# Prompt masks added on VectorE, in one operation with the queries' factor and the maximum, in a hybrid decoder step on one core

## The reference, cut to what matters

```python
logits = jnp.einsum('qngd,qknd->qngk', qg, ks).astype(jnp.float32) * (HEAD_DIM ** -0.5)
logits = jnp.where(valid[:, None, None, :], logits, -jnp.inf)
p = jax.nn.softmax(logits, axis=-1).astype(vs.dtype)
return jnp.einsum('qngk,qknd->qngd', p, vs).reshape(n_q, H_A * HEAD_DIM)
```

## Time and profile before

| | |
|---|---|
| median of 3 runs | 643.3 us (642.88 to 644.36) |
| profiled execution, own time | 640.95 us |
| its span | 639.3 us |
| granted TensorE clock | 1.00 |
| busy: TensorE, VectorE, ScalarE, GpSimd | 98%, 64%, 47%, 24% of the span |
| attention steps 8 to 23 | 287 to 375 us of the span |

### The profile page before, as it was taken

The page is one execution under the profiler, slowest core; times in us unless marked ns, Lnnn a source line. Parts: engine busy times, 40 slices in busy tenths (PEclk is TensorE's granted clock), DMA queues, the critical chain, the costliest instruction groups (busy, mean ns, idle before and its releaser), DMA issues.

```text
span 639.3 us, 13025 instructions
## 1 busy us (share of the span) xinstructions
PE 628.2 (98%) x4822; PEld 608.6 (95%) x4822; DVE 408.8 (64%) x671; ACT 298.3 (47%) x480; POOL 156.4 (24%) x211
## 2 busy tenths in 40 slices
PE   8999999999999999999999999999999999999998
PEld 6999999999999998888878899999999999999998
DVE  5765656565455568486999738868565656564441
ACT  7644444444334356455545667555444444443330
POOL 1477775000011227367412200260000000000000
PEclk9999999999999999999999999999999999999999
DMA  8777676545544556534232324544545454555530
GB/s 327 259 229 242 198 237 201 188 129 184 179 169 156 171 168 209 183 117 129 67 108 91 103 97 136 187 140 165 164 142 188 138 191 137 182 150 193 177 107 19
DMA packets 34906, 104.79 MB, mean 164 GB/s; under 512 B 6064, under 2 KB 8752, under 8 KB 34864
## 3 DMA queue, kind: packets, MB, share of 16 engines
q1 hardware_dynamic: 30432, 97.98, 46.3%
q0 software_dynamic: 3616, 4.73, 2.4%
q10 hardware_dynamic: 816, 1.51, 0.7%
HBM read 100.21 MB, written 1.70 MB: 159 GB/s over the span
## 4 chain that ended last, share of the span: by engine, by line
PE 86%; DVE 4%; DMA 2%; ACT 2%; SPq 2%; POOL 2%; issue 1%; ACTq 0%; POOLq 0%
PE ps L1190 27%; PE ps L1192 26%; PE ps L1191 26%; DVE wlo L863 1%; SPq L485 1%; DMA x<-in_x 1%; ACT whi L626 1%; PE ps L1322 1%; DVE acc L1034 1%; PE ps L1354 1%; PE ps L1385 1%; PE ps L1395 1%; DMA kv<-kv 1%; PE ps L1306 1%; PE ps L1214 0%
## 5 line engine op out<-in xcount | busy, mean ns | idle before, releaser
L863 DVE TENSOR_TENSOR wlo<-raw,whi 128x1024 fp32r<-128x1024 f32 (+2 forms) x180 | 221.3, 1234 | 125.8 <-ACT whi L626 125.5
L1190 PE MATMUL ps<-nhi,whi 128*128 128x288 f32 (+1 forms) x944 | 283.3, 300 | 1.6 <-DVE kv L1093 0.8
L1191 PE MATMUL ps<-nlo,whi 128*128 128x288 f32 (+1 forms) x944 | 278.5, 295 | 0.0
L1192 PE MATMUL ps<-nhi,wlo 128*128 128x288 f32 (+1 forms) x944 | 277.6, 294 | 0.0
L626 ACT ACTIVATE whi<-raw 128x1024 fp32r<-128x1024 f32 (+2 forms) x180 | 181.2, 1029 | 120.8 <-PE ps L1192 106.7
L1190 PEld LDWEIGHTS ps<-nhi,whi 128*128 128x128 f32 (+1 forms) x944 | 176.5, 187 | 6.7 <-issue 2.6
L1192 PEld LDWEIGHTS ps<-nhi,wlo 128*128 128x128 f32 (+1 forms) x944 | 177.4, 188 | 0.0
L1191 PEld LDWEIGHTS ps<-nlo,whi 128*128 128x128 f32 (+1 forms) x944 | 176.9, 187 | 0.3
L1190 PE MATMUL ps<-hhi,whi 128*128 128x288 f32 x336 | 99.5, 296 | 0.0
L1191 PE MATMUL ps<-hlo,whi 128*128 128x288 f32 x336 | 99.1, 295 | 0.0
L1192 PE MATMUL ps<-hhi,wlo 128*128 128x288 f32 x336 | 98.8, 294 | 0.0
(11 more groups left out here) (185 smaller groups left out, 681.5 us busy)
## 6 DMA issues: line engine op xcount, KB each, us to landing
raw<-in_weights SPq DMA_DIRECT2D x164, 512.0 KB, 3.5
raw<-in_weights SPq DMA_DIRECT2D x16, 384.0 KB, 3.4
raw<-in_weights SPq DMA_DIRECT2D x4, 256.0 KB, 5.4
kt<-in_cache_kidx_a POOLq DMA_DIRECT2D x32, 32.0 KB, 3.0
kt<-in_cache_k_b POOLq DMA_DIRECT2D x16, 64.0 KB, 3.1
kt<-in_cache_k_a POOLq DMA_DIRECT2D x32, 32.0 KB, 3.0
vb_pg<-in_cache_v_b POOLq DMA_DIRECT2D x16, 64.0 KB, 3.3
cst<-in_constants ACTq DMA_DIRECT2D x1, 948.0 KB, 7.9
```

Of the source, the lines that this page charges most:

```text
L863: nc.vector.tensor_tensor(wlo[:, v % NU, 0:nk, 0:w], raw[:, v % NR, 0:nk, 0:w], whi[:, v % NU, 0:nk, 0:w].bitcast(F32), ALU.subtract).then ...
L1190: nc.tensor.matmul(out[0:w, 0:N], h, hi, start=start and i == 0, stop=False)
L1191: nc.tensor.matmul(out[0:w, 0:N], h, lo, start=False, stop=False)
L1192: ins = nc.tensor.matmul(out[0:w, 0:N], l, hi, start=False, stop=stop and done is not False and i == len(ks) - 1)
```

## The change

The mask matmuls of the prompt steps are gone; the heads' matmuls start their banks themselves. VectorE takes each head's logits out of PSUM, adds the mask from SBUF, multiplies by the negated factor (`rq_neg`, made once for each kind at steps 8 and 16) and takes the minimum, all in one operation that writes the result to `probs` and the minimum to `nmax`. There is one such operation per head, two in a step of form 1 and four in form 0, where one reduction and one small product covered all heads of a step. ScalarE makes the exponential in place in `probs`, with scale -1. The searches write their masks in fp32 over `acc1` and `acc0`. The bf16 copies `idb`, `causalb`, `sel1` and `sel0` and their casts are gone. The sample steps (form 2) keep their mask matmuls and the reduction.

The waits follow: VectorE waits for the top-k mask and for the transposes of the step two before (its buffer of `probs`), TensorE waits for VectorE's maxima of the pair before in place of its exponentials; up to step 8 and at step 16 it still waits for the exponentials.

```diff
@@ logits (TensorE)
-                if m:
+                if 0 < m <= 8 or m in (16, 24):
                     pe.wait_ge(soft_done, m)
+                elif m:
+                    pe.wait_ge(max_done, m - 8)
...
-                if kind == DSA and i == 0:
-                    pe.wait_ge(sel_ready, {1: 1, 0: 2, 2: 3}[form])
+                if kind == DSA and form == 2:
+                    pe.wait_ge(sel_ready, 3)
...
-                    if kind != IDX:
-                        mask = ((causalb[:] if kind == MOBA else sel1[:]) if form == 1
-                                else (causalb[:, P:2 * P] if kind == MOBA else sel0[:]))
-                        for bank in banks:
-                            nc.tensor.matmul(bank[:, :].rearrange("p (h k) -> p h k", h=nh), idb[:],
-                                             mask.unsqueeze(1).to_broadcast([P, nh, w]), start=True, stop=False)
...
-                                                   k_new[rows_, 0:w], start=kind == IDX,
-                                                   stop=kind == IDX or j == nh - 1)
+                                                   k_new[rows_, 0:w], start=True, stop=True)
@@ attend (VectorE)
-                    dve.wait_ge(logits_done, m + 1)
-                    nc.vector.tensor_reduce(nmax[:, 4 * m:4 * m + nh], ps[m % 2][:, 0:nh * w].rearrange("p (h k) -> p h k", h=nh),
-                                            AX, ALU.max, negate=True).then_inc(max_raw, 1)
-                    dve.wait_ge(max_raw, m - 7)
                     if m == 8 or m == 16:
                         dve.wait_ge(rq_ready, 2 * kind)
-                    nc.vector.tensor_tensor(nmax[:, 4 * m:4 * m + nh], nmax[:, 4 * m:4 * m + nh], q_scales(m), ALU.mult)\
-                        .then_inc(max_done, 1)
+                        link(nc.vector.tensor_scalar(rq_neg[:, kind - 1, :], rq[:, kind - 1, 0:2 * HEADS], -1.0, None, ALU.mult))
+                    dve.wait_ge(logits_done, m + 1)
...
+                        if kind == DSA and i == 0:
+                            dve.wait_ge(sel_ready, 2 - form)
+                        if m >= 10:
+                            dve.wait_ge(probsT_done, m - 9)
...
+                        for h in range(nh):
+                            ins = nc.vector.tensor_tensor_reduce(
+                                probs[:, m % 2, h * w:(h + 1) * w], ps[m % 2][:, h * w:(h + 1) * w], prompt_mask(kind, form),
+                                q_scales(m)[:, h:h + 1], 3.0e38, ALU.add, ALU.min, nmax[:, 4 * m + h:4 * m + h + 1])
+                        ins.then_inc(max_done, 1)
@@ attend (ScalarE)
-                        ins = nc.scalar.activation(probs[:, m % 2, h * w:(h + 1) * w], ps[m % 2][:, h * w:(h + 1) * w],
-                                                   ACT.Exp, bias=nmax[:, 4 * m + h:4 * m + h + 1], scale=q_scales(m)[:, h:h + 1],
-                                                   accum_out=rsum[:, 4 * m + h:4 * m + h + 1])
+                        ins = nc.scalar.activation(probs[:, m % 2, h * w:(h + 1) * w],
+                                                       ps[m % 2][:, 0:w] if form == 2 else probs[:, m % 2, h * w:(h + 1) * w],
+                                                       ACT.Exp, bias=nmax[:, 4 * m + h:4 * m + h + 1],
+                                                       scale=q_scales(m) if form == 2 else -1.0,
+                                                       accum_out=rsum[:, 4 * m + h:4 * m + h + 1])
```

More of the change, by code:

```diff
@@ L281, in build @@
         cst = new("cst", [P, C_ALL])
-        idb = new("idb", [P, P], BF16)
-        causalb = new("causalb", [P, 2 * P], BF16)
         gains = new("gains", [P, GAIN_ROWS])
@@ L303, in build @@
         best = new("best", [P, 8])
-        sel1 = new("sel1", [P, 2 * P], BF16)
-        sel0 = new("sel0", [P, P], BF16)
         sel_s = new("sel_s", [NS_TOK, NK_S], BF16)
@@ L313, in build @@
         rq = new("rq", [P, 2, 3 * HEADS])
+        rq_neg = new("rq_neg", [P, 2, 2 * HEADS])
         rsel = new("rsel", [P, 2, HEADS])
@@ L364, in build @@
         qz_zero, qz_ready = [sem(s) for s in "qz_zero qz_ready".split()]
-        (logits_done, max_raw, max_done, soft_done, rinv_ready, probs_ready, probsT_done, probsT_ready) = [sem(s) for s in
-            "logits_done max_raw max_done soft_done rinv_ready probs_ready probsT_done probsT_ready".split()]
+        (logits_done, max_done, soft_done, rinv_ready, probs_ready, probsT_done, probsT_ready) = [sem(s) for s in
+            "logits_done max_done soft_done rinv_ready probs_ready probsT_done probsT_ready".split()]
         pv_done, out_hi, out_lo = [sem(s) for s in "pv_done out_hi out_lo".split()]
@@ L430, in q_scales, with prompt_mask @@
             step = head_of(kind, 1, 0) - head_of(kind, 0, 0)
-            return rq[:, kind - 1, c0:c0 + step * (len(blocks) - 1) + 1:step]
+            return rq_neg[:, kind - 1, c0:c0 + step * (len(blocks) - 1) + 1:step]
+        def prompt_mask(kind, form):
+            return ((c_(C_CAUSAL, 2 * P) if kind == MOBA else acc1[:]) if form == 1
+                    else (c_(C_CAUSAL + P, P) if kind == MOBA else acc0[:]))
         def out_views(t, bank, kind, form):
@@ L906, in _ @@
             dve.wait_ge(consts_in, 16)
-            nc.vector.tensor_copy(idb[:], c_(C_ID, P)).then_inc(masks_ready, 1)
-            nc.vector.tensor_copy(causalb[:], c_(C_CAUSAL, 2 * P)).then_inc(masks_ready, 1)
             def pair(f, p, it=0):
@@ L981, in _ @@
             vp = first["P"]
-            searches = ((acc1, TOPK_PROMPT // 8, sel1, c_(C_CAUSAL, 2 * P), 0),
-                        (acc0, TOPK_PROMPT // 8, sel0, c_(C_CAUSAL + P, P), 0),
+            searches = ((acc1, TOPK_PROMPT // 8, acc1, c_(C_CAUSAL, 2 * P), 0),
+                        (acc0, TOPK_PROMPT // 8, acc0, c_(C_CAUSAL + P, P), 0),
                         (acc_s, -(-TOPK_SAMPLE // 8), sel_s, c_(C_MASKS, NK_S, NS_TOK), TOPK_SAMPLE % 8))
@@ L1009, in attend @@
                     nh, w = {1: (2, 2 * P), 0: (4, P), 2: (1, NK_S)}[form]
-                    dve.wait_ge(logits_done, m + 1)
-                    nc.vector.tensor_reduce(nmax[:, 4 * m:4 * m + nh], ps[m % 2][:, 0:nh * w].rearrange("p (h k) -> p h k", h=nh),
-                                            AX, ALU.max, negate=True).then_inc(max_raw, 1)
-                    dve.wait_ge(max_raw, m - 7)
                     if m == 8 or m == 16:
                         dve.wait_ge(rq_ready, 2 * kind)
-                    nc.vector.tensor_tensor(nmax[:, 4 * m:4 * m + nh], nmax[:, 4 * m:4 * m + nh], q_scales(m), ALU.mult)\
-                        .then_inc(max_done, 1)
+                        link(nc.vector.tensor_scalar(rq_neg[:, kind - 1, :], rq[:, kind - 1, 0:2 * HEADS], -1.0, None, ALU.mult))
+                    dve.wait_ge(logits_done, m + 1)
+                    if form == 2:
+                        link(nc.vector.tensor_reduce(nmax[:, 4 * m:4 * m + 1], ps[m % 2][:, 0:w], AX, ALU.max, negate=True))
+                        nc.vector.tensor_tensor(nmax[:, 4 * m:4 * m + 1], nmax[:, 4 * m:4 * m + 1], q_scales(m), ALU.mult)\
+                            .then_inc(max_done, 1)
+                    else:
+                        if kind == DSA and i == 0:
+                            dve.wait_ge(sel_ready, 2 - form)
+                        if m >= 10:
+                            dve.wait_ge(probsT_done, m - 9)
+                        else:
+                            dve.wait_ge(score_ps, 2)
+                        for h in range(nh):
[3 more added lines that the diff above has]
+                        ins.then_inc(max_done, 1)
                 if m == 8:
@@ L1289, in logits @@
                 if m == 8:
-                    pe.wait_ge(masks_ready, 5)
-                if kind == DSA and i == 0:
-                    pe.wait_ge(sel_ready, {1: 1, 0: 2, 2: 3}[form])
+                    pe.wait_ge(masks_ready, 3)
+                if kind == DSA and form == 2:
+                    pe.wait_ge(sel_ready, 3)
                 if m == 0:
```

## The result

| | before | after |
|---|---|---|
| median of the runs | 644.01 us (642.88 to 645.79, 8 runs) | 638.76 us (637.77 to 641.55, 8 runs) |
| profiled execution, own time | 640.95 us | 638.3 us |
| its span | 639.3 us | 636.3 us |
| its mean granted TensorE clock | 1.00 | 0.997 |

The ratio is 0.9931, with a 95% interval of 0.9911 to 0.9951. The kernel is faster by about 4.4 us (3.2 to 5.7), outside the range forecast, on the side that had been given 0.15. Note that the two traces differ by 2.65 us only, the medians by 5.25: half of that cannot be seen by laying the traces side by side.

The account below looks back on a forecast made before the run. TensorE holds 86% of the chain, but VectorE bounds slots 18 to 21. All 2.7 us of masks saved and 0.95 more go into TensorE's waits, so 643.3 becomes 644.3 us, range 642.3 to 647.6.

Parts of the forecast that it names:

- the side that had been given 0.15: Whole kernel: chance that it comes out faster, the two faster cases lying below the range.
- the mechanism: Rival, slot 18: VectorE's weight comes before GpSimd's products, head 2.4 us earlier, kernel 641.9 us; chance 0.08.
- step 1 of the sum: Head of the chain, slot 18's weight: only slot 16's masks lie ahead, so -0.54 us.
- The price of the fused operation: VectorE's pairs: 0.36 us per 128x128 operation and 0.49 per 128x256, with 0.09 for reading the accumulator.
- The pair of slot 20: VectorE, slot 20: eight fused operations against 1.60 us, +1.28 (0.72 to 2.72).
- the pairs of four: VectorE, slots 16, 18, 24, 26: four fused operations against 1.60 us, +0.36 each (0.12 to 1.08).
- The exponentials: ScalarE, reading SBUF in place of PSUM with a constant factor: no change, 0.05 us either way for each.
- Slot 21 was left at +0.74: TensorE leaving slot 21: -0.54 from the head plus 1.28 from slot 20, 0.74 us later.
- Behind slot 21 the forecast went to +0.95: TensorE after slots 24 to 29: masks off, waits of 1.13 and 0.4 us added, +0.95 us in all.
- The dear operation: Rival, VectorE's pairs: accumulator read only once the operation drains, 0.45 and 0.58 us, kernel 646.1; chance 0.38.
- masks in full: Rival: VectorE's pairs cost no more than 1.60 us, sum ends at -1.4, kernel 641.9; chance 0.07.
- the cancelling case: Rival, whole kernel: masks and longer pairs cancel to within 0.5 us, 643.3; chance 0.47 together with the forecast.

Follow-up runs that it names:

- masks off: Kernel before with its twelve prompt mask matmuls left out and nothing put in their place: 637.28 us, ratio 0.9911.
- the filled wait: Kernel before with ten matmuls, results thrown away, in the two waits ahead of slot 21's transposes: 641.13 us, ratio 0.9951.
- the order forced back: Kernel after with one wait: VectorE makes slot 18's weight only when GpSimd's products of steps 10 and 11 have ended; 643.98 us, ratio 1.0023.
- the small delay: Kernel before with one unread GpSimd fill of 128x320 between slot 18's reciprocal roots and its two products: 638.96 us, ratio 0.9926.
- before again: Kernel before, unaltered, traced a second time: span 642.5 us at a clock of 0.995.
- order alone: Kernel before with one wait: slot 18's GpSimd products start only when VectorE has made that slot's weight; 638.45 us, ratio 0.9926.
- search behind: Kernel after with one of three search steps of slots 20 and 26 moved behind the slot's reciprocals: 638.56 us, ratio 0.9916.
- after with weight first: Kernel after with a wait that puts slot 18's GpSimd products behind VectorE's weight: 637.58 us, ratio 0.9909.
- masks kept: Kernel after with the mask matmuls still issued on TensorE, identity and mask cast as before: 644.64 us, ratio 1.0017.

## Why the prediction was wrong, step by step

**The order at slot 18, the step that failed.** The prediction had the mechanism as a rival, with its place, and gave it 0.08, because "both hang on the same slot and shift alike". They do not. The weight needs `whi`, and ScalarE can write that only when TensorE has ended the unit of slot 18 itself, whose buffer it takes, and that unit stands behind slot 18's own masks; GpSimd's train hangs on slot 17. So step 1 of the sum, "Only slot 16's masks lie ahead of that" and "Slot 18's and 20's 0.86 of masks just make TensorE wait longer", was wrong for slot 18. GpSimd's train did not bring its 0.54 either: less the 0.45 ahead of slot 16, the products started 0.18 earlier (303.54 against 304.17), behind a weight of slot 17 that took 1.58 us, 1.23 before. The trace of before had the weight's path: its chain of waits, one step further back than the earlier trace rows begins, comes from TensorE's unit (start us, us, what):

```profile
302.17 0.13 PE ps L1191
302.31 0.15 PE ps L1192
...
302.54 1.07 ACT whi L626
...
303.62 3.65 DVE wlo L863
```

With the masks off, the same chain comes through the exponentials, and TensorE's unit is no longer late:

```profile
301.39 0.65 ACT probs L757 x2
302.04 0.96 ACT whi L626
...
303.02 1.43 DVE wlo L863
```

The weight's lead grew by 0.30, from 0.55 to 0.85, where 0.09 would have done. The quicker exponentials, which then release the weight, bring another 0.2 in after. The prediction's price for the turn, 2.4 us, was too high on the path: weight 2.01 less, the rotary product behind it 0.24 more, so 1.77. Its time for that rival, 641.9, was 3.1 too long even so, and the next term is why.

**The granted clock, a term that was not in the sum.** The profile showed a clock of 1.00, and the sum has no term for the clock: the 2.35 us between that run and the median were noted and not followed up. Three of four runs of before have a mean clock as low as the one traced again, where some seven microseconds at half clock follow the 2.29 us wait. The wait was thus worth its own length and about 3 us more. By the medians, before to the filled wait is 2.9 us, mostly of clock, and from there to after 2.4, mostly of path. This also explains, to some tenths, why the traces differ by 2.65 and the medians by 5.25.

**The price of the fused operation** was mis-sized: 0.36 and 0.49 forecast, 0.27 and 0.405 measured, under the low ends of 0.29 and 0.43 too. The 0.09 for reading the accumulator was the error; plain operation plus factor, 0.21 + 0.06 and 0.35 + 0.05, is what came. The pair of slot 20 is +0.57 in place of +1.28, the pairs of four +0.02 in place of +0.36. That VectorE gains nothing held. The Trainium skill's page "VectorE: DVE Perf Modes", section on the TRN2 errata, would give an estimated 0.26 and 0.39 for the operation. The trace agrees within 0.02 from one start to the next; the recorded lengths, 0.34 and 0.48, are 0.08 and 0.09 above it. Of the 0.13 that the page would give for the one-column read nothing is seen, since the read is 0.08 long and lies beside the next operation.

**The exponentials**, taken as unchanged with 0.05 either way, took all of the 0.05: from one start to the next 0.49 us in place of 0.54 (256 columns) and 0.39 in place of 0.44 (128). The mean length is 443 ns in the line below, 510 before.

```profile
L758 ACT ACTIVATE probs<-probs,nmax 128x256 f32<-128x256 f32 (+1 forms) x32 | 14.2, 443 | 14.9 <-DVE nmax L1027 14.9
```

**The sum again**, on the trace, from slot 16 on. Slot 21 was left at +0.74 by forecast and at -2.34 + 0.45 = -1.89 in fact. Of these 2.63 us the order accounts for 2.01 - 0.24 = 1.77 (weight and rotary product), the fused operations of slot 20 for 0.71, an earlier weight for 0.15. Behind slot 21 the forecast went to +0.95 and the kernel to -2.55, 0.87 more, of which the pairs of slots 24 and 26, 0.34 cheaper each, are 0.68: slot 27 waited 0.39 in place of 1.13, and slot 29 not at all. `rq_neg` cost 0.2 at slot 24 as said, and no wait appeared ahead of the logits.

**The rivals.** The dear operation (0.38) was wrong, masks in full (0.07) did not decide: with the order forced back the change is worth nothing (ratio 1.0023), close to the cancelling case. That time, 643.98, lies in the forecast's own region of 642.9 to 644.6, but in part by luck: the fused operations were cheaper than forecast, the forced order is harsher than the natural one, and the clock was low in every run. What the change takes where the natural old order stays was not run.

## What to carry to other kernels

When two engines meet at an exclusive resource, follow back what each of them hangs on, to the tenth of a microsecond, before saying that they shift alike; where the margin is 0.1 us, write the order down with a semaphore. Take the clock of several runs, not of one profile: a wait of TensorE can cost more behind its end than in its length, and a gap between the profiled run and the median is a reading, not scatter. A change's gain may have nothing to do with what it removes: undo the suspected cause alone before crediting the change.

## What the runs showed of the hardware

- An operation that writes a minimum out is two instructions on VectorE, and the second, 0.08 us long, costs nothing: fused operations of 128x128 start every 0.27 us, of 128x256 every 0.405.
- Of VectorE with two SBUF operands and GpSimd, one waits for the other's end: a weight took 3.65 us beside two products and 1.23 where the products were held back. The Trainium skill's page "SBUF — State Buffer", section on who interferes with whom, says that whoever issues first keeps the other out. That it is a matter of order, the trace agrees. Taken by the recorded starts, three traces disagree: a weight that starts 0.54 to 0.56 us ahead of the products still comes last. That GpSimd takes the resource some 0.6 us ahead of the products' recorded start, or holds it until then for the roots before, would explain it and was not shown. Against the second speaks the small delay: the fill stands between roots and products there, and the weight still ends 0.59 us after the products' start.
- TensorE's clock, full when slot 21's wait began, was at half from about 321.5 to 328 us behind a wait of 2.29 us in two parts (before again), and from about 317, inside a wait of 2.92 that ended at 318.36 (old order forced). The kernels whose trace shows 0.66 us of waiting or less there (order alone, masks off, small delay, search behind, after with weight first) had no mean clock under 0.997, in 35 runs; of after, with 1.24, two of eight runs stood at 0.995, and where their clock fell no trace shows.
- There is an earlier stretch at half clock in some runs, within 258 to 264 us in the profiled run of after (PEclk 0.50 at 260 to 262), about 278 to 282 in four others. It can shift the order at slot 18: in the two of them whose kernels otherwise had the old order (masks kept, wait filled) the weight led by 0.64 and 0.68 us and went first. What sets it off was not tried.
